# Expert blocks in three streams with a weight set each, repeated loads predicated off, rows gathered two blocks ahead

## What is computed

```python
grp = argmax(h @ rg_w + rg_b)                       # one of 4 groups
top_val, top_idx = top_k(expert logits of that group, 2)   # 2 of its 8 experts
gate = p_grp * softmax(top_val)
# the 1024 assignments are sorted by expert; for each token t and pick j:
out[t] += gate[t, j] * ((silu(h[t] @ w_gate[e]) * (h[t] @ w_up[e])) @ w_down[e])
```

## Time and profile before

| what | value |
|---|---|
| median of 3 runs | 2205.27 us (2200.18 to 2217.95) |
| profiled execution, its own time | 2201.77 us |
| its span | 2200.5 us |
| PE busy | 1882.6 us, 86% |
| DMA moved | 396.53 MB, mean 180 GB/s |
| HBM read, written | 369.42 MB, 26.48 MB |
| expert stage, first product to last | 1547.2 to 2163.7 us of the span |

### The profile page before, as it was taken

One profiled execution on the slowest core, in us unless ns is written; L12 is line 12 of the kernel. 1 busy time (PEld: TensorE's weight loads), 2 busy tenths in 40 slices (PEclk: granted clock), 3 DMA queues, 4 the chain that ended last, 5 costly groups with the idle time before them and its releaser, 6 DMA issues. The chain is left out here.

```text
span 2200.5 us, 23528 instructions
## 1 busy us (share of the span) xinstructions
PE 1882.6 (86%) x8450; PEld 1297.7 (59%) x8450; DVE 841.8 (38%) x1143; ACT 406.0 (18%) x734; POOL 968.6 (44%) x492
## 2 busy tenths in 40 slices
PE   6999999899997999999997999674877787877872
PEld 4888888787775788888884776553222232322321
DVE  5444433311545674444437977834100000000003
ACT  3111100001454321111003355231110000100001
POOL 5888878576442788888872422110000000000001
PEclk9999999999999999999998999886899998988986
DMA  3333372332111233333221211018699999999995
GB/s 127 95 95 95 118 312 94 125 95 86 52 55 39 79 94 95 97 97 107 98 91 48 86 58 58 29 36 342 222 394 396 391 404 405 404 401 393 402 400 190
DMA packets 61919, 396.53 MB, mean 180 GB/s; under 512 B 7344, under 2 KB 7728, under 8 KB 47536
## 3 DMA queue, kind: packets, MB, share of 16 engines
q1 hardware_dynamic: 47808, 354.96, 44.1%
q10 hardware_dynamic: 9872, 26.80, 3.2%
q0 software_dynamic: 4192, 14.16, 2.0%
HBM read 369.42 MB, written 26.48 MB: 180 GB/s over the span
## 5 line engine op out<-in xcount | busy, mean ns | idle before, releaser
L265 POOL TENSOR_TENSOR weights_hi_parts<-ring,ones 128x1024 fp32r<-128x1024 f32 (+1 forms) x176 | 356.3, 2024 | 309.3 <-PE bank L448 139.5
L267 POOL TENSOR_TENSOR ring_parts<-ring,weights_hi_parts 128x1024 fp32r<-128x1024 f32 (+1 forms) x176 | 473.7, 2692 | 13.8
L1690 PE MATMUL bank<-big,work 128*64 128x512 f32 x1168 | 296.1, 651 | 101.1 <-DMA big<-w_up_in 96.5
L448 PE MATMUL bank<-attention_buffers_parts,weights_hi_parts 128*128 128x512 f32 x832 | 329.4, 396 | 27.9 <-POOL ring_parts L267 17.6
L448 PE MATMUL bank<-state_parts,weights_hi_parts 128*128 128x512 f32 x832 | 326.9, 393 | 0.0
L448 PE MATMUL bank<-attention_buffers_parts,ring_parts 128*128 128x512 f32 x832 | 326.8, 393 | 0.0
L1690 PEld LDWEIGHTS bank<-big,work 128*64 128x64 f32 x1168 | 107.7, 150 | 282.0 <-issue 262.1
L1655 POOL TENSOR_TENSOR small<-small 128x1 f32<-128x1 f32 x37 | 7.1, 193 | 562.6 <-DVE small L1606 543.6
L1675 DVE COPY work<-bank 128x512 f32<-128x512 f32 x37 | 25.6, 691 | 552.7 <-PE bank L1601 552.7
L419 PE MATMUL bank<-big_parts,weights_hi_parts 128*128 128x512 f32 x704 | 217.0, 389 | 1.2 <-POOL ring_parts L267 1.2
L448 PEld LDWEIGHTS bank<-attention_buffers_parts,weights_hi_parts 128*128 128x128 f32 x832 | 158.0, 190 | 65.0 <-POOL ring_parts L267 17.6
(11 more groups left out here) (333 smaller groups left out, 2564.8 us busy)
## 6 DMA issues: line engine op xcount, KB each, us to landing
ring<-wdense_in SPq DMA_DIRECT2D x176, 512.0 KB, 3.6
big<-w_up_in SPq DMA_DIRECT2D x37, 2048.0 KB, 25.0
big<-w_gate_in SPq DMA_DIRECT2D x36, 2048.0 KB, 19.9
state<-w_down_in SPq DMA_DIRECT2D x36, 2048.0 KB, 26.0
ring<-wff_in SPq DMA_DIRECT2D x32, 704.0 KB, 4.1
y_rows<-big ACTq DMA_DIRECT2D x1, 12288.0 KB, 42.1
y_rows<-ring ACTq DMA_DIRECT2D x74, 128.0 KB, 8.9
big<-strips_in ACTq DMA_DIRECT2D x1, 3072.0 KB, 12.5
```

Source lines behind the costliest of these rows:

```text
L265: po.tensor_tensor(hi, raw, ones[:, 0:1].to_broadcast([128, words]), ALU.mult).then_inc(PO.sem, 1)
L267: po.tensor_tensor(lo, raw, hi.bitcast(F32), ALU.subtract) \
L448: m = pe.matmul(out, x, y_, start=j + n == 0, stop=j == len(pairs) - 1 and n == len(ts) - 1)
L1690: m = pe.matmul(banks[2][m_ * BS:(m_ + 1) * BS, :], xet[:, k * BS:(k + 1) * BS], gate_up[m_][:, k * D_EXP:(k + 1) * D_EXP], start=k == 0, ...
```

## The change

The blocks keep their size and what is computed in them. What changes:

- **Three weight sets** (`sets`), of the same memory as before; block c uses set c mod 3. The list of all blocks, now with all blocks of an expert behind one another, is cut into three streams of equal length, 13 here, and the streams are interleaved: block c is number c div 3 of stream c mod 3. That makes 39 blocks, two of them empty. By the tables' arithmetic and the counts above the experts of blocks 0 to 38 are 0 1 2 | 3 11 24 | 4 12 25 | 5 13 26 | 6 14 27 | 7 15 28 | 8 17 29 | 9 18 30 | 9 19 30 | 9 20 30 | 10 21 31 | 10 23 - | 11 24 -, where a dash is an empty block.
- **Predicated loads**: a second table, `need`, says whether the block's expert differs from that of the block three earlier and the block isn't empty. SP reads expert and need from SBUF for each load of gate and up and again for each load of down, four register reads a block, and passes `need` to the load as its condition. By the list it is 0 for blocks 24, 26, 27, 29, 33, 35 and 38.
- **When loads are issued**: gate and up of block c behind PE_GU of block c - 3; down of block c - 1 behind the down product of block c - 4, which now runs in the slot of block c - 3.
- **PE's order in a slot**: gate and up of block c, the next rows' transposes, down of block c - 1, transposes of c's products. Gate and up products alternate over three banks (before: one), results over three (before: two).
- **Rows two blocks ahead**: three buffers `xe`, three `idx`; the first three gathers are issued together, then each one as soon as its buffer has been turned.
- **Tables**: the two big comparisons are gone. The expert of each block comes from a ones-matmul over a one-hot table (L448 on PE, 8 matmuls of 52 columns), read by a few small DVE instructions ahead of the first rows' copy.
- Engines run loops of three blocks, with the first slot and the last two or three written out ahead of and behind them.

```diff
-SLOT_COLS = MAX_BLOCKS + 2
+SETS = 3
+SLOT_COLS = MAX_BLOCKS + 4
 ...
-    s_gath = sem("block_rows_gathered")
-    s_wexp = [[sem(f"expert_weights_{n}_{b}") for b in range(2)] for n in ("gate", "up", "down")]
-    s_first = [sem(f"first_expert_{n}") for n in ("gate", "up", "down")]
+    s_gath = [sem(f"block_rows_gathered_{b}") for b in range(SETS)]
+    s_wexp = [[sem(f"expert_weights_{n}_{b}") for b in range(SETS)] for n in ("gate", "up", "down")]
 ...
-    wg, wu, wd = big[:, 0:2 * WE], big[:, 2 * WE:4 * WE], state
-    first_w = (ring[:, RING * SLOT - WE:RING * SLOT], big[:, 4 * WE:5 * WE], att[:, 0:WE])
     assert RING * SLOT - WE >= 1024 + 8 * BS and 5 * WE <= BIG - 8 * T
+    sets = ((ring[:, RING * SLOT - WE:RING * SLOT], big[:, 4 * WE:5 * WE], att[:, 0:WE]),
+            (big[:, 0:WE], big[:, 2 * WE:3 * WE], res[:, 0:WE]),
+            (big[:, WE:2 * WE], big[:, 3 * WE:4 * WE], nrm[:, 0:WE]))
 ...
-    def load_expert(m, b, e):
-        buf = (wg, wu, wd)[m]
-        sp.dma_start(buf[:, b * WE:(b + 1) * WE], experts_d[m][bass.ds(e, 1), :, :].rearrange("a p c -> p (a c)")) \
-            .then_inc(s_wexp[m][b], 16)
+    def load_expert(m, b, e, needed=None):
+        if needed is None:
+            d = sp.dma_start(sets[b][m], experts_d[m][e])
+        else:
+            d = sp.dma_start(sets[b][m], experts_d[m][bass.ds(e, 1), :, :].rearrange("a p c -> p (a c)"), cond=needed)
+        d.then_inc(s_wexp[m][b], 16)
     for m in range(3):
-        sp.dma_start(first_w[m], experts_d[m][0]).then_inc(s_first[m], 16)
-    for b in range(2):
+        load_expert(m, 0, 0)
+    for b in (1, 2):
         for m in range(2):
-            load_expert(m, b, b + 1)
+            load_expert(m, b, b)
     sp.wait_ge(PE.sem, PE.n)
-    load_expert(2, 0, 1)
+    load_expert(2, 1, 1)
     sp.wait_ge(s_hrow, NT * 16)
-    load_expert(2, 1, 2)
+    load_expert(2, 2, 2)
 ...
+    for b in range(SETS):
+        PO.wait(DV.run(take_rows(b, slice(b, b + 1))))
+        gather(b)
+    exp1, exp_i, need = sm(SLOT_COLS), sm(SLOT_COLS), sm(SLOT_COLS)
+    PE.wait(experts_placed)
+    s = PE.step(product(banks[3][:, 0:SLOT_COLS],
+                        [(ones[:, :], oh_exp[:, c * SLOT_COLS:(c + 1) * SLOT_COLS]) for c in range(C2)]))
+    DV.step(dv.memset(need[:, 0:SETS].bitcast(I32), 0))
     DV.wait(s)
-    PE.wait(DV.run(dv.tensor_copy(xet, banks[0][:, :])))
-    dv.wait_ge(s_gath, 16)
-    DV.run(take_rows(slice(1, 2)))
-    exp_i, exp_f, exp_g = sm(MAX_BLOCKS), sm(MAX_BLOCKS), sm(MAX_BLOCKS)
-    before_it = hi_raw[:, D:D + MAX_BLOCKS * 32].rearrange("p (b e) -> p b e", e=32)
-    def ends_before(dst, blocks, ends, op):
-        DV.run(dv.tensor_tensor(before_it, over_last(blocks, MAX_BLOCKS, 32),
-                                ends.unsqueeze(1).to_broadcast([128, MAX_BLOCKS, 32]), op))
-        DV.run(dv.tensor_reduce(dst, before_it, axis=AX.X, op=ALU.add))
-    DV.run(dv.tensor_scalar(exp_g, iota_f[:, 0:MAX_BLOCKS], firsts, None, ALU.subtract))
-    ends_before(exp_f, iota_f[:, 0:MAX_BLOCKS], first, ALU.is_gt)
-    ends_before(exp_i, exp_g, last_b, ALU.is_ge)
-    DV.run(dv.tensor_scalar(exp_g, exp_g, 0.0, float(-N_EXP), ALU.is_ge, ALU.mult))
-    DV.run(dv.tensor_tensor(exp_f, exp_f, exp_i, ALU.add))
-    DV.run(dv.tensor_tensor(exp_f, exp_f, exp_g, ALU.add))
-    tables = DV.run(dv.tensor_scalar(exp_i.bitcast(I32), exp_f, float(N_EXP - 1), None, ALU.min))
+    DV.run(dv.tensor_copy(exp1, banks[3][:, 0:SLOT_COLS]))
+    DV.step(dv.tensor_scalar(exp_i.bitcast(I32), exp1, -1.0, 0.0, ALU.add, ALU.max))
+    changed = work[:, 2560:2560 + SLOT_COLS - SETS]
+    DV.run(dv.tensor_tensor(changed, exp1[:, SETS:SLOT_COLS], exp1[:, 0:SLOT_COLS - SETS], ALU.not_equal))
+    tables = DV.run(dv.scalar_tensor_tensor(need[:, SETS:SLOT_COLS].bitcast(I32), exp1[:, SETS:SLOT_COLS], 0.0, changed,
+                                            ALU.is_gt, ALU.mult))
+    pe.wait_ge(s_gath[0], 16)
+    s = PE.step(turn_rows(0))
+    DV.wait(s)
+    dv.tensor_copy(xet, banks[0][:, :]).then_inc(DV.sem, 1)
+    take_rows(0, slice(3, 4)).then_inc(DV.sem, 2)
+    DV.n += 3
 ...
-    with sp.Fori(1, n_pairs["sp"]) as i:
-        for b in range(2):
-            e = sp.value_load(exp_i[0:1, bass.ds(i * 2 + b + 1, 1)].bitcast(I32), min_val=0, max_val=N_EXP - 1)
-            for m, k in enumerate((PE_GU, PE_GU, PE_D)):
-                sp.wait_ge(PE.sem, at_step(PE, k, i, b - 2))
-                load_expert(m, b, e)
 ...
+    def gate_up(i, c, rows_next=True):
+        b = c % SETS
+        pe.wait_ge(DV.sem, at_step(DV, DV_X, i, c - 1))
+        for m_ in range(2):
+            pe.wait_ge(s_wexp[m_][b], i * 16 + (16 * (c // SETS) + 16))
+        for k in range(KD):
+            if k == KD - 1 and rows_next:
+                pe.wait_ge(s_gath[(c + 1) % SETS], i * 16 + (16 * ((c + 1) // SETS) + 16))
+            for m_ in range(2):
+                m = pe.matmul(first_products[b][m_ * BS:(m_ + 1) * BS, :], xet[:, k * BS:(k + 1) * BS],
+                              sets[b][m_][:, k * D_EXP:(k + 1) * D_EXP], start=k == 0, stop=k == KD - 1)
+        m.then_inc(PE.sem, 1)
+    def next_rows(c):
+        turn_rows(c % SETS).then_inc(PE.sem, 1)
+    def down(i, c, steps=1):
+        b = c % SETS
+        pe.wait_ge(DV.sem, at_step(DV, DV_MUL, i, c))
+        pe.wait_ge(s_wexp[2][b], i * 16 + (16 * (c // SETS) + (32 if b == 2 else 16)))
+        for k in range(4):
+            for half in range(2):
+                m = pe.matmul(results[b][half * BS:(half + 1) * BS, :], het[:, k * BS:(k + 1) * BS],
+                              sets[b][2][:, k * D + half * 512:k * D + half * 512 + 512], start=k == 0, stop=k == 3)
+        m.then_inc(PE.sem, steps)
 ...
+    def dve_rows(i, c):
+        dv.wait_ge(PE.sem, at_step(PE, PE_X, i, c))
         dv.tensor_copy(xet, banks[0][:, :]).then_inc(DV.sem, 1)
-        dv.wait_ge(AC.sem, at_step(AC, AC_SILU, i, b))
-        dv.tensor_tensor(het3, hg3, turned_h[:, :, 1, :], ALU.mult).then_inc(DV.sem, 1)
-        dv.wait_ge(s_gath, i * 32 + 16 * (b + 3))
-        take_rows(bass.ds(i * 2 + b + 3, 1)).then_inc(DV.sem, 1)
+        take_rows((c + 4) % SETS, bass.ds(i * SETS + (c + 4), 1)).then_inc(DV.sem, 1)
+    def dve_mul(i, c, steps=1):
+        dv.wait_ge(AC.sem, at_step(AC, AC_SILU, i, c))
+        dv.tensor_tensor(het3, hg3, turned_h[:, :, 1, :], ALU.mult).then_inc(DV.sem, steps)
+    def load_first(i, c):
+        e = sp.value_load(exp_i[0:1, bass.ds(i * SETS + c, 1)].bitcast(I32), min_val=0, max_val=N_EXP - 1)
+        needed = sp.value_load(need[0:1, bass.ds(i * SETS + c, 1)].bitcast(I32), min_val=0, max_val=1)
+        sp.wait_ge(PE.sem, at_step(PE, PE_GU, i, c - SETS))
+        for m in range(2):
+            load_expert(m, c % SETS, e, needed)
+    def load_down(i, c):
+        e = sp.value_load(exp_i[0:1, bass.ds(i * SETS + c, 1)].bitcast(I32), min_val=0, max_val=N_EXP - 1)
+        needed = sp.value_load(need[0:1, bass.ds(i * SETS + c, 1)].bitcast(I32), min_val=0, max_val=1)
+        sp.wait_ge(PE.sem, at_step(PE, PE_D, i, c - SETS + 1))
+        load_expert(2, c % SETS, e, needed)
 ...
+    with sp.Fori(0, laps["sp"]) as i:
+        for c in range(SETS, 2 * SETS):
+            load_first(i, c)
+            load_down(i, c - 1)
+    load_down(laps["sp"], SETS - 1)
+    gathers_begun = PO.n
+    with po.Fori(0, laps["po"]) as i:
+        for c in range(SETS):
+            po.wait_ge(PO.sem, i * SETS + (gathers_begun + c))
+            po.wait_ge(DV.sem, at_step(DV, DV_IDX, i, c - 1))
+            po.tensor_tensor(zo, zc, zc, ALU.add).then_inc(PO.sem, 1)
+            gather(c)
 ...
+    gate_up(0, 0)
+    next_rows(1)
+    turn_products(0, 0, 2)
+    with pe.Fori(0, laps["pe"]) as i:
+        for c in range(1, SETS + 1):
+            gate_up(i, c)
+            next_rows(c + 1)
+            down(i, c - 1)
+            turn_products(i, c)
+    gate_up(laps["pe"], 1)
+    next_rows(2)
+    down(laps["pe"], 0)
+    turn_products(laps["pe"], 1)
+    gate_up(laps["pe"], 2, rows_next=False)
+    down(laps["pe"], 1, 2)
+    turn_products(laps["pe"], 2)
+    down(laps["pe"], 2)
```

260 lines of the change are left out of this document (130 added, 130 removed).

## The result

| what | before | changed |
|---|---|---|
| median of the runs shown | 2202.72 us (4 runs, 2197.04 to 2217.95) | 2143.26 us (4 runs, 2138.81 to 2145.26) |
| profiled execution, its own time | 2201.77 us | 2141.47 us |
| its span | 2200.5 us | 2140.2 us |
| DMA moved | 396.53 MB | 365.89 MB |

The ratio is 0.9717, with an interval of 0.9664 to 0.9769: 2.8% faster, inside the range. The span is 60.3 us shorter where 69.5 was worked out, and the median 2143 where 2135 was said.

What follows compares the result with a forecast made beforehand. Transfers were taken to bound the expert stage. A start 21.6 us earlier and 15 fewer matrices, against 14 blocks at PE's speed and a longer last slot, gave 69.5 us less: span 2131.0, time about 2135, range 2112 to 2172.

Steps and rivals of the forecast that it cites:

- The start: Start of the expert stage: with the big table rows gone, block 0 begins at 1539.1 instead of 1547.2.
- The price of a load up to block 23: Weights' queue: 61 matrices at 5.75 us, 350.5 us from 1548.6, so block 23's w_up lands at 1899.1.
- DMA starts 21.6 us earlier: First load behind the preloads: SP may issue it at 1548.6 instead of 1570.25.
- it could cost a microsecond or two, for which I put nothing: Start of the stage: three gathers at once instead of one might cost a microsecond or two, counted as nothing.
- The number of loads, and where they are dropped: Expert blocks: 29 loaded instead of 34 behind the preloads, 15 matrices fewer, all seven drops from block 24 on.
- Block 24 on at PE's speed: Tail of the stage: PE is the bound, 14 slots (24 to 37) of 11.7 us, 163.8 us in all.
- the closest: Block 25 in the tail: its w_up lands at 1922.1 and is wanted at 1925.0, the smallest margin.
- DMA well under 1: Sign of a right forecast: from block 24 on, DMA share well under 1, with 11.7 us slots and clock 1.00.
- The end: Last slot: block 38 starts at 2077.1, last product ends at 2094.2, then 36.8 us to the span's end.
- the 4.3 at which SP would have been the bound: Rival, SP's register reads: from 4.3 us a read, tail slots reach 18.3 us, over 1% slower than before; 4%.
- that rival: Rival: code is fetched at every return of PE's loop, up to 65 us, giving 2200, or 2155 to 2200; 6%.
- that one: Rival: small gaps keep the clock down in the tail, PE's slots lengthen, 35 us in all, giving 2170; 10%.

Runs made afterwards that it cites:

- the first experiment: The changed kernel, but every block that has rows loads its weights, none dropped: 2199.62 us against 2203.66 for the kernel before (ratio 0.999).

## Why the prediction was right, point by point

*The start.* Block 0 was said to start at 1539.1 and did so at 1536.2, 2.9 earlier; its gather was issued 3.2 earlier (1524.24 for 1527.46), since this execution reached the stage sooner. That part is luck: in the other profiled executions of kernels with this start the gather was issued between 1523.75 and 1533.77. The step itself, 12 us behind the gather, was right. The small tables lie under the gather.

*The first load.* Said for 1548.6, it was issued at 1545.09. Right.

*The price of a load up to block 23: the term that was mis-sized.* 61 matrices by 5.75 us were 350.5 us; they took 1906.22 - 1545.09 = 361.1. The error is in the first seven: w_up of block 5 landed at 1595.28, 50.2 us behind the first issue, where 7 x 5.75 is 40.3. That is 9.9 of the 10.6 us; the other 54 took 310.8, which is 5.76 each. "DMA starts 21.6 us earlier" counted from when SP may issue, not from when the queue is free, and "it could cost a microsecond or two, for which I put nothing" was the other half. The windows of the changed kernel and of the kernel before, ahead of the first load:

```profile
1530.00:1535.00 5.00, 0.79 (x7) 0.79 (x8) 0.00 (x0) 0.00 (x0) 0.00 (x0) 0.50 1.05 314
1535.00:1540.00 5.00, 4.15 (x16) 1.38 (x16) 0.74 (x2) 0.00 (x0) 1.09 (x2) 0.57 1.00 305
1540.00:1545.00 5.00, 5.00 (x28) 1.59 (x25) 0.00 (x0) 0.17 (x1) 0.00 (x0) 1.00 0.98 285
```

```profile
1530.00:1535.00 5.00, 0.00 (x0) 0.00 (x0) 0.00 (x0) 0.00 (x0) 0.00 (x0) 0.50 1.00 353
1535.00:1540.00 5.00, 1.12 (x8) 0.93 (x8) 1.56 (x4) 0.00 (x0) 0.00 (x0) 0.50 0.98 391
1540.00:1545.00 5.00, 0.00 (x0) 0.00 (x0) 4.90 (x4) 0.00 (x0) 0.00 (x0) 0.50 1.01 429
```

The DMA share is full in both. But the three gathers land 9.9, 12.8 and 16.8 us behind their issues and a fourth is issued at 1536.60, so two or three are under way for most of this time, and the engines bring 285 to 314 GB/s instead of 353 to 429. From 1520 to 1545 the weights' queue moved 7.68 MB where it had moved 9.96 before. These 2.28 MB are 1.1 matrices, some 6 us. Counted from 1493, ahead of the preloads, which began 2.5 us sooner in this execution, it is 18.43 MB for 20.35: the preloads are 1.92 MB, some 5 us, behind where they were. That was the place for the term: what the queue still holds at 1548.6, and what the gathers take from it. It is near the 7.7 us that the late first load showed; the other 2.2 us are there from an empty queue too, 42.5 for 40.3.

*The number of loads, and where they are dropped.* 15 matrices less, all behind block 23; right in number and place, and the key of the forecast. Without them the kernel is where it was before (the first experiment).

*Block 24 on at PE's speed.* Right: no wait for weights there, clock 1.00. The slot was 11.83 for 11.7, 2 us over 14 slots. Block 25 was called the closest; it didn't wait here. In the kernel with three result buffers, the same in its loads, the step from block 24 to 25 is 12.5 us, a wait of 0.6: close indeed. "DMA well under 1" in the tail was wrong until 2050: the share was 0.95 and 1.01 there. SP is three blocks ahead and issues whatever it may, so a full queue doesn't say that PE waits for it.

*The end.* From the last slot's start (2086.21) to the end of its last product (2103.50) it is 17.3 us for 17.1, and 36.7 for 36.8.

*What was put at nothing.* Two register reads lie between 1567.04 and 1568.15 in the chain of the kernel with the late first load, some 0.55 us each, an eighth of the 4.3 at which SP would have been the bound. A dropped issue is 0.07 to 0.09. The queues of instructions brought 2 packets each from 1550 to 2104 us, and slots at the loop's returns are as long as the others, so code for the longer body isn't fetched at each return and that rival fell. The clock in the tail was 1.00, so that one fell too.

Put together: 2131.0 forecast, less 3.5 for the first load that came earlier, plus 10.6 for the price, about 2 for the slots, gives 2140.1; the span is 2140.2. The terms partly cancel, and the 3.5 us that cancel are mostly luck, so the forecast of 2135 missed by less than its largest term did.

## What to carry to other kernels

A load that is dropped pays only where somebody waits for the queue: lay the engine's slots and the queue's loads side by side, block by block, before counting what dropping saves, and then place the drops so that they lie in front of the loaded stretches. An earlier start of a queue counts from when the queue is empty, not from when the issue is free to go; look at the DMA share in the windows behind that point. And a transfer that is issued behind a step of one block and wanted in the next closes a ring with the engine that waits for it (here 20.5 us, with rows one block ahead instead of two). Once the ring is longer than what the queue needs for a block, it sets the pace, and the full queue is no longer the bound.

## What the runs showed of the hardware

- **A dropped load is in the profile's counts but not in its bytes.** The page lists w_up 39 times at 2048 KB, though only 32 were brought by the queue, and gives 384.36 MB read from HBM, more than before (369.42), while all queues together moved 365.89 MB, less than before (396.53). The line on HBM reads counts the loads by their issues: the kernel that loads no weight behind the preloads has the same 384.36 MB in it, while its weights' queue brought 141.05 MB instead of 323.51. With a condition on a load only the queues' bytes can be read:

```profile
big<-w_up_in SPq DMA_DIRECT2D x39, 2048.0 KB, 33.1
```

- **It costs 0.07 to 0.10 us of SP's queue**, against 0.34 for one that goes, and its semaphore counts as if the data had come.
- **Gathers take more of the DMA engines than their bytes.** At a share of 1.00 the rate was 285 to 314 GB/s with mostly two or three gathers of 0.26 MB under way and 353 to 429 with one or none. Most of the loss is in the loads beside them: from 1520 to 1545 the weights' queue took 88.0% of the engines' time for 7.68 MB, 11.5% a MB, where before it took 97.5% for 9.96 MB, 9.8% a MB. Why, no run shows.
- **The same kernel's transfers scatter by about 1% between executions** (530.5 and 524.0 us for the same 31 blocks), enough to swallow an edit worth 6 us.
